# A mixture-of-experts block layer on one NeuronCore: gated expert rows added straight to the output, and the two expert biases applied differently

## The reference

```python
x_new = x + g_a * merge(ret_branch(ret_l, rg), diff_branch(diff_l), ga, gb)
x_new = x_new + g_f * _moe(_modulate(_rmsnorm(x_new, norm2_g), sh_f, sc_f), ...)

def _moe(h, router_w, router_b, w1, b1, w2, b2):
    ...
    logits = (xt @ router_w + router_b).astype(jnp.float32)
    top_val, top_idx = lax.top_k(logits, TOP_K)          # 4 of 32 experts
    gate = jax.nn.softmax(top_val, axis=-1)
    ...
    hh = xblk @ w1[e] + b1[e]                            # 1024 -> 2048
    glu = jnp.minimum(hh[:, :D_FF], SWIGLU_LIMIT)
    lin = jnp.clip(hh[:, D_FF:], -SWIGLU_LIMIT, SWIGLU_LIMIT)
    act = glu * jax.nn.sigmoid(SWIGLU_ALPHA * glu) * (lin + 1.0)
    return act @ w2[e] + b2[e]                           # 1024 -> 1024
    ...
    y = jax.ops.segment_sum(yb * row_gate[:, None], row_tok, ...)
```

## Time and profile before

| | us |
|---|---|
| median of 3 runs | 2360.9 (2360.1 to 2362.79) |
| the profiled execution, its own time | 2360.16 |
| its span, first to last instruction | 2358.4 |
| PE busy | 2289.2 (97%) |
| DVE busy | 1676.1 (71%) |
| ACT busy | 1257.1 (53%) |
| POOL busy | 325.3 (14%) |

### The profile page before, as it was taken

One profiled execution on the slowest core, in us unless ns is written; L12 is line 12 of the kernel. 1 busy time (PEld: TensorE's weight loads), 2 busy tenths in 40 slices (PEclk: granted clock), 3 DMA queues, 4 the chain that ended last, 5 costly groups with the idle time before them and its releaser, 6 DMA issues.

```text
span 2358.4 us, 29945 instructions
## 1 busy us (share of the span) xinstructions
PE 2289.2 (97%) x10471; PEld 1806.5 (77%) x10471; DVE 1676.1 (71%) x1522; ACT 1257.1 (53%) x1198; POOL 325.3 (14%) x315
## 2 busy tenths in 40 slices
PE   7999999999999999998799999999999999999995
PEld 3868678685887787787678888888888888888884
DVE  4525353343646666748599889889889889889885
ACT  4212122121234624623377777777777777777773
POOL 2000000000211132001412111111121111111111
PEclk9999999999999999999799999999999999999997
DMA  8322314131231021134699999999999999999995
GB/s 290 130 85 90 125 44 153 36 107 71 90 108 36 20 88 36 54 125 162 252 352 388 389 377 392 384 379 394 382 377 390 386 377 391 388 376 392 386 376 179
DMA packets 135843, 563.47 MB, mean 239 GB/s; under 512 B 11494, under 2 KB 19830, under 8 KB 101694
## 3 DMA queue, kind: packets, MB, share of 16 engines
q1 hardware_dynamic: 123624, 518.14, 57.1%
q0 software_dynamic: 11280, 38.11, 6.1%
q10 hardware_dynamic: 872, 6.31, 0.7%
HBM read 535.61 MB, written 26.90 MB: 239 GB/s over the span
## 4 chain that ended last, share of the span: by engine, by line
PE 93%; DVE 4%; DMA 1%; ACT 1%; issue 1%; SPq 0%; POOL 0%; ACTq 0%; POOLq 0%; DVEq 0%
PE ps L1992 89%; PE ps L2472 1%; PE ps L2480 1%; PE ps L2306 1%; DMA ar<-in_x 0%; PE ps L2248 0%; DMA raw<-in_w_mod 0%; DVE nmx L1645 0%; PE ps L2194 0%; DVE wlo L1854 0%; DVE wlo L1294 0%; DMA acc_d<-ar,cur 0%; DVE ar L1986 0%; DVE ar L1984 0%; DVE cst L1757 0%
## 5 line engine op out<-in xcount | busy, mean ns | idle before, releaser
L1992 PE MATMUL ps<-whi,yhi 128*128 128x512 f32 x1088 | 383.0, 417 | 0.0
L1854 DVE TENSOR_TENSOR hlo<-raw,hhi 128x2048 fp32r<-128x2048 f32 x132 | 302.5, 2292 | 48.5 <-ACT hhi L1187 48.3
L1992 PE MATMUL ps<-hhi,yhi 128*128 128x512 f32 x1056 | 335.9, 389 | 0.0
L1854 DVE TENSOR_TENSOR wlo<-raw,whi 128x2048 fp32r<-128x2048 f32 x132 | 299.3, 2288 | 39.9 <-ACT whi L1187 39.9
L1294 DVE TENSOR_TENSOR wlo<-raw,whi 128x2048 fp32r<-128x2048 f32 x60 | 137.4, 2289 | 227.3 <-ACT whi L898 226.1
L1187 ACT ACTIVATE hhi<-raw 128x2048 fp32r<-128x2048 f32 x132 | 253.2, 1918 | 81.3 <-PE ps L1992 81.3
L1187 ACT ACTIVATE whi<-raw 128x2048 fp32r<-128x2048 f32 x132 | 253.1, 1919 | 64.3 <-PE ps L1992 64.3
L1992 PE MATMUL ps<-ar 128*128 128x128 f32 (+5 forms) x1014 | 241.8, 433 | 11.3 <-ACT ar L1176 4.4
L1992 PE MATMUL ps<-whi,hhi 128*128 128x512 f32 x608 | 239.9, 395 | 1.9 <-DVE hlo L1599 1.1
L1992 PEld LDWEIGHTS ps<-whi,yhi 128*128 128x128 f32 x1088 | 207.1, 190 | 39.5
L1992 PE MATMUL ps<-whi,hlo 128*128 128x512 f32 x608 | 237.0, 390 | 0.0
(11 more groups left out here) (278 smaller groups left out, 3886.5 us busy)
## 6 DMA issues: line engine op xcount, KB each, us to landing
raw<-in_exp_w SPq DMA_DIRECT2D x264, 1024.0 KB, 6.6
ar<-in_exp_w SPq DMA_DIRECT2D x132, 1024.0 KB
raw<-in_w_in SPq DMA_DIRECT2D x44, 1024.0 KB, 5.0
raw<-in_w_mod SPq DMA_DIRECT2D x22, 1024.0 KB, 5.5
raw<-in_w_br_ret SPq DMA_DIRECT2D x8, 1024.0 KB, 5.1
ar<-in_x SPq DMA_DIRECT2D x8, 512.0 KB, 11.6
raw<-in_w_br_diff SPq DMA_DIRECT2D x4, 1024.0 KB, 5.1
raw<-in_w_out SPq DMA_DIRECT2D x4, 1024.0 KB, 8.1
```

What stands on the lines that cost most here:

```text
L1854: V.tensor_tensor(e_wlo[j % ESPL], e_raw[s], e_whi[j % ESPL].bitcast(F32), ALU.subtract).then_inc(e_lo, 1)
L1992: return pe.matmul(out, lhsT, rhs, start=start, stop=stop, skip_group_check=skip)
```

## The change

Five things change together.

1. The gated rows of a block are also multiplied by `g_f`, in one DVE instruction instead of two on ACT, and are added straight onto the output array. The output array is first filled with `x_new` (four stores from SP, after the first chunks of expert weights). The scratch array `acc_d`, its loads back and the last multiplications and additions go.
2. The second bias is multiplied by `g_f` as well. Its eight matmuls stand inside `up(0)`, two after each of the chunks 2 to 5, and its rows go out as four indirect accumulating DMAs from POOL.
3. The first bias is held in two fp32r parts: a matmul has 64 rows. The parts for banks 2 and 3 (`b` 0 and 1) lie on partitions 0 to 63, those for banks 4 and 5 on 64 to 127, and the four matmuls stand together at the head of `up`, in the order 0, 2, 1, 3. `b1` is loaded by four DMAs of 32 x 4 KB instead of one of 32 x 8 KB, twice the bytes.
4. Gathers and scatters take a bound: rows that pad a block are left out.
5. A small ACT instruction with Silu stands ahead of the first block's `glu`.

```diff
+        def bias_split(dve, tl):
+            src = F(A_BSRC, D)
+            dve.wait_ge(b_loaded, 64)
+            tl.did(V.tensor_scalar(src[64:128, :], src[64:128, :], 1.0, None, ALU.add))
             tl.wait()
+            part = [src[:, q * COL:(q + 1) * COL].rearrange("p (a n) -> p a n", a=2) for q in range(2)]
+            for q in range(2):
+                tl.did(V.tensor_copy(bias[q], part[q]))
             tl.wait()
+            for q in range(2):
+                for r in (slice(32, 64), slice(96, 128)):
+                    tl.did(V.tensor_tensor(bias[q][r], part[q][r], bias[q][r].bitcast(F32), ALU.subtract))
             tl.wait()
...
             sp.dma_start(F(A_GFB, D), mod_d[0:1, 5 * D:6 * D].broadcast_to((P, D))).then_inc(vec2, 16)
-            sp.dma_start(bsrc[0:N_EXPERTS, 0:2 * D], a["exp_b1"]).then_inc(b_loaded, 16)
+            for r in range(4):
+                sp.dma_start(F(A_BSRC, D)[32 * r:32 * r + 32, :], a["exp_b1"][:, r // 2 * D:(r // 2 + 1) * D]).then_inc(b_loaded, 16)
...
             load_w1(0, 0, 4)
+            for t in range(LT):
+                sp.dma_start(a["out"][t * P:(t + 1) * P, :], F(A_XN, LT, D)[:, t, :]).then_inc(stored, 16)
...
             def scatter(i):
-                pool.wait_ge(y_out, i * 2 + 2)
+                pool.wait_ge(y_out, i + 1)
                 hold()
-                pool.indirect_dma_start(acc_d, bass.IndirectOffsetOnAxis(ap=cur[:, 0:1], axis=0),
-                                        F(A_Y, D), None, compute_op=ALU.add).then_inc(y_added, 16)
+                pool.indirect_dma_start(a["out"], bass.IndirectOffsetOnAxis(ap=cur[:, 0:1], axis=0),
+                                        F(A_Y, D), None, bounds_check=L - 1, oob_is_err=False,
+                                        compute_op=ALU.add).then_inc(y_added, 16)
...
             next_sel(0, 1)
+            pool.wait_ge(stored, 16 * LT)
+            for t in range(LT):
+                pool.wait_ge(gb_out, 2 * t + 2)
+                hold()
+                pool.indirect_dma_start(a["out"], bass.IndirectOffsetOnAxis(ap=lval[:, t * TOP_K, 0:1], axis=0),
+                                        bias_rows[t], None, bounds_check=L - 1, oob_is_err=False,
+                                        compute_op=ALU.add).then_inc(acc_init, 16)
             next_gather(0, 2)
...
-            def give_y(i, last):
-                act.wait_ge(cur_ready, i + 1)
-                act.wait_ge(e_used, last + 1)
-                for c in range(2):
-                    act.activation(F(A_Y, D)[:, c * COL:(c + 1) * COL], ps[:, 6 + c, :], ACT.Copy,
-                                   scale=cur[:, 1:2].bitcast(F32)).then_inc(y_out, 1)
...
             gate_exp(3)
-            act.wait_ge(b2_loaded, 16)
+            x_high(0)
+            act.wait_ge(b2_scaled, 1)
...
-            x_high(0)
-            for j in range(ESPL, FIRST):
-                hi_e(0, j)
-            act.wait_ge(acc_init, 16 * LT)
+            act.activation(junk32[:, 0:1], ones[:, 0:1], ACT.Silu)
             glu(0)
...
             lo(OUT0, 0, 0, 2)
-            bias_thirds(dve, tl, bias, 0)
+            bias_split(dve, tl)
...
             lo(OUT0, 0, 0, 3)
-            bias_thirds(dve, tl, bias, 1)
             for t in range(LT):
                 new_x(1, t)
...
+            dve.wait_ge(b2_loaded, 16)
+            V.tensor_tensor(b2, b2, F(A_GFB, D)[0:N_EXPERTS, :], ALU.mult).then_inc(b2_scaled, 1)
...
+            def give_y(i, last):
+                dve.wait_ge(cur_ready, i + 1)
+                dve.wait_ge(e_used, last + 1)
+                V.scalar_tensor_tensor(out=F(A_Y, D), in0=psf[:, 6 * COL:8 * COL], scalar=cur[:, 1:2].bitcast(F32),
+                                       in1=F(A_GFB, D), op0=ALU.mult, op1=ALU.mult).then_inc(y_out, 1)
...
                 act_low(i - 1)
+                if not isinstance(i, int):
+                    give_y(i - 2, chunk(i - 1, MOE_N - 1))
                 for j in range(ESPL, MOE_N - 1):
                     lo_e(i, j)
...
-            for t in range(LT):
-                s = F(A_XG if t == 0 else A_Y if t == 1 else A_GS if t == 2 else A_HT, D)
-                dve.wait_ge(acc_back[t], 16)
-                fin.did(V.tensor_tensor(s, s, F(A_GFB, D), ALU.mult))
-                fin.wait()
-                V.tensor_tensor(xn[:, t, :], xn[:, t, :], s, ALU.add).then_inc(res_ready, 1)
+            give_y(end, chunk(end + 1, MOE_N - FIRST - 1))
...
+            def up(i, between=None):
                 pe.wait_ge(sel_ready, i + 1)
+                pe.wait_ge(e_lo, chunk(i, 0) + 1)
+                for b in (0, 2, 1, 3):
+                    r = slice(b // 2 * 64, b // 2 * 64 + 64)
+                    last = mm(ps[:, 2 + b, :], sel[r, :], bias[b % 2][r], True, False)
+                last.then_inc(sel_used, 1)
...
-                        if kk == 0:
-                            last = mm(o, sel[0:96, :], bias[0:96, cols], True, False)
-                            if b == 3:
-                                last.then_inc(sel_used, 1)
...
+            def bias_part(kk):
+                t = kk - 2
+                if not 0 <= t < LT:
+                    return
+                if t:
+                    pe.wait_ge(gb_out, 2 * t)
+                else:
+                    pe.wait_ge(gb_lo, 2)
+                for c in range(2):
+                    last = mm(ps[:, 6 + c, :], dense3[:, t * P:(t + 1) * P], b23[:, c * COL:(c + 1) * COL], True, True)
+                last.then_inc(gb_done, 1)
+
+            up(0, bias_part)
```

More of the change, by code:

```diff
@@ L1218, in item @@
                 if isinstance(i, int):
-                    act.sem_inc(y_out, 2)
-                else:
-                    give_y(i - 2, chunk(i - 1, MOE_N - 1))
+                    act.sem_inc(y_out, 1)
                 act_high(i - 1)
@@ L1276, in _ @@
             end = act.value_load(count_i[0:1, 1:2], min_val=N_EXPERTS - 1, max_val=MAX_BLOCKS - 1)
-            give_y(end - 1, chunk(end, MOE_N - 1))
             act_high(end)
@@ L1280, in _ @@
                 hi_e(end + 1, j)
-            give_y(end, chunk(end + 1, MOE_N - FIRST - 1))
         @block.vector
@@ L1969, in _ @@
                 lo_e(1, j)
-            with dve.Fori(1, N_EXPERTS) as i:
+            item(1)
+            with dve.Fori(2, N_EXPERTS) as i:
                 item(i)
@@ L1976, in _ @@
             act_low(end)
+            give_y(end - 1, chunk(end, MOE_N - 1))
             for j in range(AHEAD, ESPL):
                 lo_e(end + 1, j)
-            fin = Steps(dve, tail, tl.k)
-            for t in range(LT):
-                s = F(A_XG if t == 0 else A_Y if t == 1 else A_GS if t == 2 else A_HT, D)
-                dve.wait_ge(acc_back[t], 16)
-                fin.did(V.tensor_tensor(s, s, F(A_GFB, D), ALU.mult))
-                fin.wait()
-                V.tensor_tensor(xn[:, t, :], xn[:, t, :], s, ALU.add).then_inc(res_ready, 1)
+            give_y(end, chunk(end + 1, MOE_N - FIRST - 1))
         @block.tensor
@@ L2444, in _ @@
             first_rows(3)
-            pe.wait_ge(dense_ready, LT)
-            for t in range(LT):
-                last = pe.transpose(ps[0:N_EXPERTS, 1, t * P:(t + 1) * P], dense[:, t, 2:2 + N_EXPERTS], ident)
-            last.then_inc(route_step, 1)
             pe.wait_ge(m_ready, 2 * LT)
@@ L2465, in _ @@
             actlo = ylo[:, 2:4, :].rearrange("p a (k n) -> p (a k) n", n=P)
-            bias = F(A_BIAS, 1024).bitcast(BF16)
             def turn_x():
```

117 lines of the change are left out of this document (45 added, 72 removed).

## The result

The changed kernel takes 2349.92 us (median of 5 runs, 2347.77 to 2352.34), the kernel before 2360.9 (2360.1 to 2362.79): a ratio of 0.995, 95% interval 0.9939 to 0.9961. It is 11 us faster where 26.4 were forecast.

What follows compares the result with a forecast made beforehand. TensorE was taken as the bound, busy 97% of the span and throughout the block loop. Terms summing to -26.4 us took 2360.16 to 2333.8; 0.7 for the median gave 2334.5 us, range 2325 to 2350.

Steps and rivals of the forecast that it cites:

- behind the last product: End of the kernel: load back, DVE work and stores go, 16.4 us, and a shorter last landing 1.5; -17.9 us.
- blocks: Bias matmuls in each `up`: four of 64 rows, side by side, take 0.84 us against 0.99; 33 x 0.15, -5.0 us.
- first bias ahead of `new_x`: Ahead of `new_x`: 5.4 us of DVE bias work goes, first norm 1.9 earlier, less 0.7 for x's later landing; -1.2 us.
- start of the first block: First gather to `up(0)`: fewer gathered rows save 1.9 us, ACT without its bias copies ahead 1.1; -3.0 us (-0.5 to -4).
- second bias in `up(0)`, table load: Eight bias matmuls inside `up(0)` cost +2.0 us; ACT's table load moving into its idle time saves 1.3.
- DVE hidden: Block loop: `give_y` on DVE delays chunk 4 about 0.2 us, hidden by some 12 us; uncovered, up to 1.22 a block.
- Both overlap rivals: 64-row matmuls in `up`: no overlap at fp32r pace, 2349.7 us, chance 0.11; overlap in part, 2339.5 us, chance 0.07.
- The 1.1 for ACT's bias copies: First block, transposes to `up(0)`: 3.35 us instead of 4.49, with ACT's bias copies no longer ahead of the high parts.
- The 1.9 for the gather: First block's gather: 72 rows of 128 move, so transposes start 4.4 x 56/128 = 1.9 us earlier.
- bounds don't save what they say: Rival on gather and scatter: skipped rows take as long; adds 1.9 + 1.5 us, 2337.9; chance 0.09.
- DVE as the bound: Rival at the head of each block: TensorE waits for DVE at chunk 4, a block takes 36.6 us, kernel 2377; chance 0.03.
- the clock: Rival in the blocks: 64-row visits make TensorE lose clock, 2.5 us a block, 83 in all, kernel 2417; chance 0.02.

## Why the prediction was wrong

| Step | forecast | measured |
|---|---|---|
| behind the last product | -17.9 | 24.5 to 15.2: -9.3 |
| last `down`, behind `give_y` of the block before | not seen | +0.8 |
| blocks | -5.0 | 33 x 0.133: -4.4 |
| first bias ahead of `new_x` | -1.2 | 43.3 to 42.4: -0.9 |
| start of the first block | -3.0 | -1.1, -0.8 and +0.5: -1.4 |
| second bias in `up(0)`, table load | +0.7 | 32.8 to 32.7: 0 |
| sum | -26.4 | -15.2 |

The measured values are the middle of all traces that have the code in question. The second row is what the last block takes beyond the others: 3.14 and 3.35 us in the two traces of before, 4.08 in the changed kernel. The traced spans fell from 2358.4 and 2361.6 to 2345.4 to 2350.2 in six kernels that end like the changed one, 13 us on average. The medians of the timed runs differ by 11.0 for the changed kernel; for the five others they lie 11.5 to 14.2 under the kernel before, timed beside them, so 11.0 is at the low end of a spread and no contradiction. Of the 2 us between 13 and the sum, the granted clock is about half (the merge's start, the half clock at 1095, `up(1)`, the last products); the rest is open.

**The tail, -17.9: the step that failed.** It is "What lies behind goes: 2358.4 - 2341.98 = 16.4 us off the end". Of these 16.4 us 7.3 are not chain but GpSimd's end, which had stood beside the chain all the time. Of the 1.5 us for a shorter landing 0.3 came (5.91 to 5.6; 5.3 to 5.8 over the other traces with this end): few rows land hardly sooner, as in the gather.

**DVE hidden: right in the loop, wrong at its end.** The argument (12 us until chunk 4 is needed) was made for a block in the middle. At the end there is no `up` to cover it: the next thing on TensorE is `down`, which needs banks 6 and 7 free, and DVE's queue is full. `give_y` moved from ACT, where it had run ahead, to the engine without a gap. TensorE waits 4.0 us for it where it had waited 3.0 for the low activations.

**Blocks: right**, mechanism and size: 0.133 against 0.15, the price of a mode 0.40 against 0.39, pairs at the pace of one product. Both overlap rivals fall.

**Start of the first block: mis-sized.** The 1.1 for ACT's bias copies is there: 3.35 us from the transposes to `up(0)`, as forecast (before 4.49). The 1.9 for the gather were taken in proportion from 4.4 us of packets with list writes and loads between them; of them 0.8 came, and 0.5 goes back ahead of the gather, to the bound's own instruction. The rival "bounds don't save what they say" was right here.

**First bias: right in kind**, 0.9 instead of 1.2. **Second bias and table load:** both terms came as forecast. The eight products take 0.234 us each, 1.9 in all. ACT's load lies in idle time now: from the end of `up(0)` to the next block's `up` it is 6.20 us instead of 7.54. `up(0)` as a whole is only 1.0 to 1.5 longer (26.3 to 26.8 us in most traces, before 25.2 and 25.3), and the granted clock in it is 0.92 to 0.94 in three of them where it was 0.90. ACT, behind the bias copies:

```profile
1173.09 1.09 ACT L1242 ACTIVATE ar<-ps 128x512 f32<-128x512 f32 x2 [2.09 <-PE ps L1979]
1174.19 1.28 ACT L1250 ACT_TABLE_LOAD   x1
...
1178.58 1.02 ACT L1190 ACTIVATE ar<-ps 128x1024 f32<-128x1024 f32 x1 [2.89 <-PE ps L1979]
```

Both other rivals, DVE as the bound and the clock, didn't come: the loop's row has TensorE at 300.00 of 300 and 1.00.

## What to carry to other kernels

When a change cuts the end off a chain, ask of every engine what it still has to do after its last instruction, and subtract only down to the latest of these: here GpSimd's close costs 6.8 us, free as long as something else runs on, and the views don't show it. Let another engine wait for GpSimd's last transfer: here that hid 3.2 us of the close, while 3.9 stayed behind the landing. A last transfer that doesn't go through GpSimd might hide it all; that wasn't tried. An argument that a step is hidden holds for the place it was made for: repeat it for the first and the last round of the loop. And before explaining a difference of 1 us between two traces, look at a second trace of the same kernel.

## What wasn't expected of the hardware

- GpSimd's closing DRAIN takes 6.77 to 6.89 us with nothing under way. Begun with its last indirect transfer not yet issued it takes 9.5 to 9.7 us and ends 3.90 us behind the landing, in each of three traces.
- TensorE's branch over the second loop of extra blocks takes 3.35 to 3.92 us in all fourteen traces.
- 64-row products on the two halves run side by side even when the program has them in the order upper, upper, lower, lower.
- A bound on an indirect gather delays its issue by 0.55 us behind the wait, and 56 of 128 rows fewer (4 KB each) bring its last packet 0.2 to 0.4 us forward.
